# V's causal convolution moved from channel-major to token-major layout in a two-layer hybrid decoder trunk

## The reference

```python
def _causal_depthwise_conv(x, w):                       # CONV_WIDTH = 4, one filter per channel
    return lax.conv_general_dilated(x, w[:, None, :], window_strides=(1,),
        padding=[(CONV_WIDTH - 1, 0)], dimension_numbers=('NWC', 'WIO', 'NWC'),
        feature_group_count=x.shape[-1])

def _gated_deltanet_mixer(h, w_in, conv_w, a_log, dt_bias, norm_w, w_out):
    proj = h @ w_in
    qkv, z, b_pre, a_pre = _split(proj, L1_SPLITS)
    qkv = jax.nn.silu(_causal_depthwise_conv(qkv, conv_w))
    q, k, v = _split(qkv, [GDN_QK_W, GDN_QK_W, GDN_V_W])    # 2048, 2048, 4096 channels
    ...   # l2 norm of q and k; 32 value heads of 128; chunked gated delta rule
    o = _head_rmsnorm(o) * norm_w
    return (o.reshape(...) * jax.nn.silu(z)) @ w_out
```

## Time and profile before

| | |
|---|---|
| median of 3 runs | 2720.18 us |
| profiled execution, own time | 2721.59 us |
| its span (first to last instruction) | 2719.8 us |
| PE busy | 2702.9 us (99%) |
| DVE busy | 1812.3 us (67%) |
| ACT busy | 1411.3 us (52%) |
| POOL busy | 95.8 us (4%) |
| DMA, mean | 188 GB/s |

### The profile page before, as it was taken

How to read it: one execution, slowest core, us unless ns; L and a number is a source line. 1 busy time by engine, 2 the same in 40 slices (tenths; PEclk the granted TensorE clock), 3 DMA queues, 4 the chain that set the end, 5 groups by cost and what they waited for, 6 DMA issues and landing times.

```text
span 2719.8 us, 37018 instructions
## 1 busy us (share of the span) xinstructions
PE 2702.9 (99%) x13170; PEld 2247.2 (83%) x13170; DVE 1812.3 (67%) x2538; ACT 1411.3 (52%) x2005; POOL 95.8 (4%) x80
## 2 busy tenths in 40 slices
PE   8999999999999999999999999999999999999998
PEld 7888888888888888888888888888888888888887
DVE  5554678666666766668797978656767666666444
ACT  5444555444444444458787778554454444444443
POOL 0000000000000000001111111000000000000000
PEclk9999999999999999999999999999999999999999
DMA  7564466666666656666464656555566666666664
GB/s 255 161 195 146 155 195 192 198 192 193 192 193 192 194 189 196 195 190 196 153 190 155 187 177 191 173 179 190 194 193 194 192 193 193 192 193 194 208 193 159
DMA packets 264735, 510.95 MB, mean 188 GB/s; under 512 B 20496, under 2 KB 21264, under 8 KB 264352
## 3 DMA queue, kind: packets, MB, share of 16 engines
q1 hardware_dynamic: 260064, 493.95, 59.5%
q0 software_dynamic: 3152, 11.57, 1.3%
q10 hardware_dynamic: 1392, 3.77, 0.4%
HBM read 503.95 MB, written 5.28 MB: 187 GB/s over the span
## 4 chain that ended last, share of the span: by engine, by line
PE 95%; DVE 3%; DMA 1%; ACT 0%; issue 0%; DVEq 0%; SPq 0%; ACTq 0%
PE acc L604 30%; PE acc L605 30%; PE acc L610 30%; PE aux L847 1%; DVE wlo L1557 1%; PE aux L691 1%; PE aux L852 1%; PE aux L841 0%; DMA wraw<-in_l_w_in 0%; DVE arena L2002 0%; PE aux L833 0%; DVE const L2002 0%; PE aux L875 0%; DVE arena L2043 0%; DVE arena L2040 0%
## 5 line engine op out<-in xcount | busy, mean ns | idle before, releaser
L1557 DVE TENSOR_TENSOR wlo<-wraw,whi 128x1024 fp32r<-128x1024 f32 x928 | 1143.1, 1240 | 705.8 <-ACT whi L1060 701.1
L1060 ACT ACTIVATE whi<-wraw 128x1024 fp32r<-128x1024 f32 x928 | 978.6, 1059 | 1091.1 <-PE acc L610 1053.5
L604 PE MATMUL acc<-whi,hT_hi 128*128 128x512 f32 x2624 | 1034.5, 394 | 2.0 <-DVE hT_lo L1749 1.2
L605 PE MATMUL acc<-whi,hT_lo 128*128 128x512 f32 x2624 | 1023.2, 390 | 0.0
L610 PE MATMUL acc<-wlo,hT_hi 128*128 128x512 f32 x2624 | 703.1, 390 | 0.5 <-DVE wlo L1557 0.5
L604 PEld LDWEIGHTS acc<-whi,hT_hi 128*128 128x128 f32 x2624 | 493.3, 188 | 104.0 <-DVE hT_lo L1749 1.5
L610 PEld LDWEIGHTS acc<-wlo,hT_hi 128*128 128x128 f32 x2624 | 492.4, 188 | 103.6 <-DVE wlo L1557 1.3
L605 PEld LDWEIGHTS acc<-whi,hT_lo 128*128 128x128 f32 x2624 | 493.6, 188 | 99.8
L604 PE MATMUL acc<-whi,arena 128*128 128x512 f32 x1072 | 417.3, 389 | 0.0
L605 PE MATMUL acc<-whi,arena 128*128 128x512 f32 x1072 | 417.2, 389 | 0.0
L610 PE MATMUL acc<-wlo,arena 128*128 128x512 f32 x1072 | 286.6, 389 | 0.0
(11 more groups left out here) (272 smaller groups left out, 1193.1 us busy)
## 6 DMA issues: line engine op xcount, KB each, us to landing
wraw<-in_l_w_in SPq DMA_DIRECT2D x304, 512.0 KB, 4.2
wraw<-in_l_w_gate SPq DMA_DIRECT2D x176, 512.0 KB, 3.9
wraw<-in_l_w_up SPq DMA_DIRECT2D x176, 512.0 KB, 4.3
wraw<-in_l_w_down SPq DMA_DIRECT2D x176, 512.0 KB, 4.4
wraw<-in_l_w_out SPq DMA_DIRECT2D x96, 512.0 KB, 4.6
arena<-decay_sums POOLq DMA_DIRECT2D x16, 512.0 KB, 5.3
o_rounds<-arena POOLq DMA_DIRECT2D x3, 1024.0 KB, 5.3
arena<-o_rounds ACTq DMA_DIRECT2D x3, 1024.0 KB, 5.6
```

The costliest lines, as they stand in the source:

```text
L604: nc.tensor.matmul(pair[m], hi[:, k, tok], wh, start=first, stop=False)
L605: nc.tensor.matmul(pair[m], lo[:, k, tok], wh, start=False, stop=False)
L1060: nc.scalar.activation(whi[:, s, :], wraw[:, s, :], ACT.Copy).then_inc(hi_done, 1)
L1557: V.tensor_tensor(wlo[:, s, :], wraw[:, s, :], whi[:, s, :].bitcast(F32), ALU.subtract).then_inc(lo_done, 1)
```

## The change

V0 and V1 are no longer turned. POOL copies each block three times by DMA from one place in SBUF to another, shifted by 1, 2 and 3 tokens (`lags`, `row_lag`); the shift goes across partitions, so each copy is one transfer of 127, 126 or 125 partitions and one small one for the tokens that cross from the first group of 128 to the second. DVE multiplies the block and its three copies by taps that SP has loaded, broadcast over all partitions (`taps`, `tap_rows`, 1 MB each), and adds the four: 7 tensor_tensor instructions of 128x1024 and one small memset (`v_conv`), at slots 5, 8 and 9 for V0 and 24, 27 and 28 for V1. ACT applies SiLU at slots 11 and 30 and scales the rows from SBUF. Four further moves come with it:

- the place for two copies and the taps is `x`, the residual, which POOL stores to HBM (2 MB) after the last block of layer 0 and loads back after the last round;
- the leaf copies into `T` go from POOL to ACT (slot 22);
- `load_o(0)` on ACT goes from slot 2 to slot 11 of the last round, `load_o(1)` and `load_o(2)` from 28 to 30; two gatings of Z move by 2 and 3 units, and a `z_out` from place 5 to 7 of its block;
- ACT writes a new V block into `qkv` only once the old one has been summed (`v_sum`).

```diff
@@ slots and taps
-Z_GATED = {1: 159, 2: 164, 3: 167, 4: 173, 5: 181, 6: 189}
+Z_GATED = {1: 159, 2: 167, 3: 169, 4: 173, 5: 181, 6: 189}
+TAPS_AT = {14: (0, V0)}
+TAPS_AT.update({ROUND_AT[r] + 18: (r, V1) for r in range(ROUNDS)})
+TAPS_AT.update({ROUND_AT[r - 1] + 36: (r, V0) for r in range(1, ROUNDS)})
+V_BLOCK = lambda r, b: 2 * r + (b == V1)
+V_STEPS, V_LAGS = 4, 2 * (CW - 1)
@@ SP
+            def taps(r, b):
+                n, col = V_BLOCK(r, b), P * conv_tile(r, b)
+                if n:
+                    sp.wait_ge(v_sum, n)
+                else:
+                    sp.wait_ge(x_stored, 16)
+                sp.dma_start(tap_rows, A["conv_rows"][:, col:col + NB].rearrange("(a w) n -> a w n", a=1).to_broadcast([P, CW, NB])
+                             ).then_inc(taps_in, 16)
@@ POOL
+            def store_x():
+                pool.wait_ge(xs_copied, 8)
+                pool.dma_start(x_dram[:, :], xflat).then_inc(x_stored, 16)
+                pool.wait_ge(x_stored, 16)
+                nc.gpsimd.memset(row_lag[0][0:1, 0, :], 0.0)
+                nc.gpsimd.memset(row_lag[1][0:2, 0, :], 0.0).then_inc(lag_zero, 1)
+            def load_x():
+                pool.wait_ge(v_sum, 2 * ROUNDS)
+                pool.dma_start(xflat, x_dram[:, :]).then_inc(x_back, 16)
+            def lags(r, b):
+                n = V_BLOCK(r, b)
+                pool.wait_ge(acc_read[b % 2], (BLOCK0["l1"] + 4 * r + b) // 2 + 1)
+                if n:
+                    pool.wait_ge(v_sum, n)
+                    pool.wait_ge(v_rows, n)
+                for lag in range(1, CW):
+                    dst = row_lag[lag - 1]
+                    pool.dma_start(dst[0:lag, 1, :], qkv[P - lag:, 0, v_cols(b)]).then_inc(v_lags, 16)
+                    pool.dma_start(dst[lag:, :, :], qkv[0:P - lag, :, v_cols(b)]).then_inc(v_lags, 16)
             def gdn(r):
...
+                lags(r, V1)
...
-                pool.wait_ge(leaf_set, LEAF_AT(r, "T"))
-                for b in range(3):
-                    pool.drain()
-                    a = nc.gpsimd.tensor_copy(T[quarter(b), :, :, quarter(b)].rearrange("p c h j -> p (c h) j"), leaf_T[quarter(b), :, :])
-                a.then_inc(t_in, 1)
...
                     decay_rows(r + 1)
+                    lags(r + 1, V0)
                     decay_columns(r + 1)
@@ PE
-                if s == 0:
-                    if r:
-                        pe.wait_ge(end_dve, END_DVE(r - 1, "o1"))
-                    conv_transposes(V0, aux[1])
...
-                if s == 10:
+                if s == 15:
                     pe.wait_ge(tok_copy, TOK_AT(r, K))
-                    token_major(V0, aux[0])
...
-                if s == 27:
-                    pe.wait_ge(kq_mask, r + 1)
-                    conv_transposes(V1, aux[0])
...
-                if s == 31:
-                    pe.wait_ge(conv_sum, TOK_AT(r, V1))
-                    token_major(V1, aux[0])
@@ ACT
+                def v_rows_silu(b):
+                    act.wait_ge(v_sum, V_BLOCK(r, b) + 1)
+                    nc.scalar.activation(flat(row_lag[2]), flat(row_lag[2]), ACT.Silu).then_inc(v_silu, 1)
...
+                if s == 22:
+                    act.wait_ge(leaf_set, LEAF_AT(r, "T"))
+                    act.wait_ge(tt_zero, r + 1)
+                    for b in range(3):
+                        a = nc.scalar.activation(T[quarter(b), :, :, quarter(b)].rearrange("p c h j -> p (c h) j"), leaf_T[quarter(b), :, :], ACT.Copy)
+                    a.then_inc(t_in, 1)
...
-                if s == 28:
-                    tap(V1)
+                if s == 30:
+                    v_rows_silu(V1)
@@ DVE
+                def v_conv(b, part):
+                    n, v = V_BLOCK(r, b), qkv[:, :, v_cols(b)]
+                    tap = lambda lag: tap_rows[:, CW - 1 - lag, :].unsqueeze(1).to_broadcast([P, M, NB])
+                    if part == 0:
+                        dve.wait_ge(taps_in, 16 * (n + 1))
+                        dve.wait_ge(v_lags, 16 * V_LAGS * (n + 1))
...
+                        V.tensor_tensor(v, v, tap(0), ALU.mult)
+                        V.tensor_tensor(row_lag[0], row_lag[0], tap(1), ALU.mult).then_inc(v_step, 1)
+                    if part == 1:
+                        V.tensor_tensor(row_lag[1], row_lag[1], tap(2), ALU.mult)
+                        V.tensor_tensor(row_lag[2], row_lag[2], tap(3), ALU.mult).then_inc(v_step, 1)
+                    if part == 2:
+                        dve.wait_ge(v_step, V_STEPS * n + 1)
+                        V.tensor_tensor(v, v, row_lag[0], ALU.add).then_inc(v_step, 1)
+                        dve.wait_ge(v_step, V_STEPS * n + 2)
+                        V.memset(row_lag[2][0:CW - 1, 0, :], 0.0)
+                        dve.wait_ge(v_step, V_STEPS * n + 3)
+                        V.tensor_tensor(v, v, row_lag[1], ALU.add).then_inc(v_step, 1)
+                    if part == 3:
+                        dve.wait_ge(v_step, V_STEPS * n + 4)
+                        V.tensor_tensor(row_lag[2], v, row_lag[2], ALU.add).then_inc(v_sum, 1)
```

More of the change, by code:

```diff
@@ L1475, in qkv_out @@
                     act.wait_ge(k_turns, r - 1)
+                elif r and q in (V0, V1):
+                    act.wait_ge(v_sum, V_BLOCK(r - 1, q) + 1)
                 elif r:
@@ L1509, in hook_l1 @@
                     qkv_out(b - 1)
[L1510 removed]
+                if j == {Z_BLOCK + 2: 5, Z_BLOCK + 3: 5, Z_BLOCK + 4: 7}.get(b, 3) and b > Z_BLOCK:
                     z_out(b - Z_BLOCK - 1)
```

87 lines of the change are left out of this document (58 added, 29 removed).

## The result

The changed kernel takes 2882.46 us (median of 4 runs, 2881.38 to 2886.28) against 2720.26 us for the kernel before on the same chip: a ratio of 1.060, 95% interval 1.0585 to 1.061. The prediction was 2734 (2716 to 2770) and is wrong by 148 us. What came is the rival "copies that run on one DMA engine", to which it gave 0.14.

The account below looks back on a forecast made before the run. PE was taken as the bound, waiting on DVE and ACT. A round: +3.3 (slot 25) - 1.74 (V1) + 1.4 (slot 30) = +3.0; four rounds +12, start +1, transfers +1: +14, giving 2734 us (2716 to 2770).

Parts of the forecast that it names:

- copies that run on one DMA engine: Rival, lag copies: 127, 126 or 125 partitions go through one engine, 13 to 178 us on top of 14; chance 0.14.
- PE's saving: PE, V0 and V1: 128 transposes fewer, 14.0 us, or 3.5 a round, 1.74 for each block.
- The sum itself: Whole kernel: +3.0 us a round, +12 for four rounds, start +1, transfers +1, together +14.
- V0 on DVE: Up to slot 25: DVE 4.4 us late, PE has 1.1 of lead, so PE 3.3 later each round.
- The term for the leaf copies: POOL's copies into T go to ACT: DVE gets 0.7 us a round back, bounds 0 and 0.7.
- V1 and slot 30: Slots 24 to 30: PE saves 1.74 us, then waits 1.4 (0 to 2.5) for ACT's last_copy behind V1's SiLU.
- Round 3: Last round: no lead, but load_o(0) moves to slot 11; 3.3 us taken as elsewhere, x's load back costs nothing.
- Start of layer 1: POOL's 2 MB store of x runs beside the weight stream: 1 us, ends 0 and 4.
- Taps and copies: Taps of 1 MB and 12 MB of copies beside the weight stream: 0 to 6 us, 1 taken.
- the one for a wrong forecast: Signs of error: 127 us rounds without wlo waits, first v_conv waiting tens of us for DMA, or start losing over 4.

Follow-up runs that it names:

- v1_three: Kernel before with V1 alone token-major, transfers and orders mended, in rounds 0 to 2; V0 and round 3 as before: 2717.58 us, ratio 0.9988.
- bare: Changed kernel without its 24 large copies, and from the second V block on taps for one partition only (V is wrong): 2751.44 us, ratio 1.0114.
- v1_only: Kernel before with V1 alone token-major in all rounds, copies cut, taps in four, SiLU late (rounds 0 to 2), k_tail after the sum: 2726.92 us, ratio 1.0023.
- bare_t_pool: As bare, with the copies of the leaf blocks into T back on POOL: 2749.88 us, ratio 1.0106.
- spread_silu_late: Changed kernel with all large copies cut into 112 partitions and a rest, V1's SiLU behind the second last_copy in rounds 0 to 2: 2765.28 us, ratio 1.0164.

## Why the prediction was wrong, step by step

The changed kernel's 162 us, taken apart by runs: the large copies in one piece 113 (2882.5 to 2769.5), the taps as one block 14, the copies in themselves 4, POOL's product beside DVE's sum 10.7, V0's work on DVE 22.9 (2740.8 to 2717.9), and -3 for all else (PE's saving, less the start and round 3). The sum is 161.6; it has to be near 162, since each term is the step from one kernel to the next (they were measured on four chips, on which the kernel before took 2720.1 to 2720.9), and in another order single terms come out otherwise (V0's work is 23.8 ahead of the change to `k_tail` and 22.9 behind it).

- **The step that failed** is the choice in the rivals: "I hold the spread for likelier because it is given for this very case". The runs showed one engine in its place: 107 of the 162 us go with one partition count, 127. The mechanism was known and priced (13 to 178 us on top of 14, 2749 to 2914; the time is in it), and no row of the kernel before spoke against it, since none had such a count. What decided was one exception in the section of the Trainium skill cited there, set against the general rule of the same section. On such ground the rival deserved far more than 0.14. Its price was near in its parts: `v_conv` waits 20.9 us at the first block, where 13 to 38 was said, and 67.9 us over all eight. A copy is 127 packets of 4 KB and not 254 of 2 KB: alone that is 127 x 0.156 = 20 us (25 said), in turns with the stream 127 x 0.235 = 30 (50 said). What it missed is that the wait isn't DVE's alone: the weights come late by the same copies (ACT's 173.8 us). And that the time lies within the rival's range is partly luck, since the "14" it stands on was 49.
- **The sum itself** would have failed as well. Without the one-engine copies it is 49 us and not 14: 2769.5 is outside the 2724 to 2752 given to it, and inside 2716 to 2770 by half a microsecond. The next points say which terms.
- **PE's saving**: right. x13042 against x13170, 128 transposes. It came through where `wlo` kept its lead (v1_three: 1.8 a round for V1).
- **V0 on DVE**: right in kind, and in size for rounds 0 to 2. The parts take 1.22 to 1.23 us each (1.15 behind the memset), the memset 0.48 (0.6 said). `bare` loses 3.8 us from the start to slot 25 of round 0, where 3.3 was said; in rounds 1 to 3 it is 4.8, 3.9 and 6.3, so round 3, for which the prediction took 3.3 too, was 3 short. Without V0's work 5.9 a round come back, which is 3.3 and PE's 1.74 with 0.9 over; PE's time at the lower clock falls with it, from 20.5 to 13.7 us, and half of that is 0.85 a round. The term for the leaf copies (0.7 a round) isn't confirmed, and neither is their full 3.71 us, which the rule cited beside it would give.
- **V1 and slot 30**: mis-sized. A saving of 0.87 at slot 31 and a wait of 1.4 were to make +0.5 there; `bare` loses 4.2 (4.5 to 8.7) in round 0. I had counted DVE's additions at 1.22 and not looked at what POOL does beside them: its product waits for slot 29 of PE, had shown POOL and DVE in each other's way, and in the same trace this product (POOL, 1321.82 us, 2.49 us long) has a single `wlo` of 2.33 us beside it on DVE (1323.07). Moving the product wins 2.7 a round. What the wait does to PE's clock had no term at all.
- **Round 3**: not priced. I noted that `load_o(0)` gets out of the way, and not that `load_o(1)` and `load_o(2)` move behind a wait and so next to the load of `x`, which was put at nothing ("where `wlo` leads by far"). Where all three are asked for within 3 us the weights are late; with `x` 10 us behind (v1_three) nothing is lost. In bare round 3 costs 11.1 us where the others cost 4 to 7; in v1_only it turns a gain into a loss. Only 3.0 of the 8.4 us there come when those loads do; the other parts were named above, and their shares weren't tested one by one.
- **Start of layer 1**: right (1.0 to 1.6 us in the table, said 1; 3.4 and 4.4 in the traces of `bare_t_pool` and `spread_silu_late`, whose edits don't touch it). **Taps and copies**: "0 to 6 us, I take 1", measured 14 + 4. The prediction left the unit behind the taps 4.4 us of slack and took 4 of delay; 1 MB lands in 9.9 us and not in twice 4.2. That ACT isn't always ready to copy at once may add to it; this wasn't measured.

Of the marks set in advance, the one for a wrong forecast was met to the letter: DVE's first `v_conv` waited tens of us for a DMA.

## What to carry to other kernels

Shifting by one partition is cheap for the engines and may be the dearest transfer of all: cut a copy whose partition count has no divisor near 16 into one that has and a small rest, before anything else is judged. When work is moved to DVE, look at what POOL runs beside it, since an addition of 1.22 us can take 2.80, and at PE's clock, since a wait of 1.9 us was followed by 6.8 us at half speed. A change with two halves should be costed by halves: here V1's wins 1.8 us a round, and V0's, ahead of the place where DVE has no lead, loses 5.9.
